# Linear-recurrence stage with its decay exponents as TensorE products and its heads interleaved

## What is computed

```python
def hgrn2_mixer(hq, hf, hi, hg, lb, out_gain):
    log_f = logaddexp(log(lb), log1p(-lb) + log_sigmoid(hf))
    k = -expm1(log_f)
    q = silu(hq)
    o = hgrn2_chunk_scan(q, k, hi, log_f)      # per head
    return rmsnorm(o, out_gain) * silu(hg)

# S_t = diag(f_t) S_{t-1} + k_t v_t^T,  o_t = S_t^T q_t, in chunks:
def step(S, (qi, ki, vi, gi)):
    b = cumsum(gi)
    o_inter = einsum('tk,kv->tv', qi * exp(b), S)
    att = einsum('tk,tsk,sk->ts', qi, exp(b_t - b_s where s <= t), ki)
    o_intra = att @ vi
    S_new = exp(b_last) * S + (ki * exp(b_last - b))^T @ vi
```

## Time and profile before

| | |
|---|---|
| three timed runs, median (lowest to highest) | 2146.06 us (2145.73 to 2147.39) |
| the profiled execution's own time | 2147.82 us |
| its span, first to last instruction | 2146.0 us |
| TensorE, VectorE, ScalarE, POOL busy | 1964.3, 1076.2, 739.0, 98.7 us |
| mean granted clock of TensorE | 0.955 |
| recurrence and first `wout` tile | 252.97 to 409.06 us |

### The profile page before, as it was taken

The page is one execution under the profiler, slowest core; times in us unless marked ns, Lnnn a source line. Parts: engine busy times, 40 slices in busy tenths (PEclk is TensorE's granted clock), DMA queues, the critical chain, the costliest instruction groups (busy, mean ns, idle before and its releaser), DMA issues.

```text
span 2146.0 us, 28165 instructions
## 1 busy us (share of the span) xinstructions
PE 1964.3 (92%) x11116; PEld 1695.4 (79%) x11116; DVE 1076.2 (50%) x1469; ACT 739.0 (34%) x1185; POOL 98.7 (5%) x106
## 2 busy tenths in 40 slices
PE   7999765799999998799999999999787989999996
PEld 7878665799999998688888877777587758888884
DVE  4643477444443446854444557676525253323334
ACT  4352333133323233342232334534435242212221
POOL 0100144100000000000000000000000020000000
PEclk9999878899999999999999999999979989999998
DMA  4211000133232322323323322222001313223221
GB/s 171 69 50 49 30 1 0 49 88 90 89 90 81 97 89 66 101 89 98 97 89 98 93 84 89 69 69 79 30 1 44 104 49 98 90 90 104 90 94 44
DMA packets 45475, 161.28 MB, mean 75 GB/s; under 512 B 4848, under 2 KB 5104, under 8 KB 45232
## 3 DMA queue, kind: packets, MB, share of 16 engines
q1 hardware_dynamic: 45216, 158.60, 23.4%
q10 hardware_dynamic: 144, 1.05, 0.1%
HBM read 155.43 MB, written 4.19 MB: 74 GB/s over the span
## 4 chain that ended last, share of the span: by engine, by line
PE 85%; DVE 7%; ACT 4%; issue 2%; DVEq 1%; DMA 0%; ACTq 0%; SPq 0%; POOL 0%; POOLq 0%
PE ps L466 72%; PE ps L836 2%; PE ps L588 2%; DVEq L1946 1%; PE ps L756 1%; PE ps L856 1%; PE ps L729 1%; DVE XE L1942 1%; DVE wlo L1778 1%; DVE W L2088 1%; PE ps L727 1%; DVE GT L2394 1%; PE ps L999 0%; DMA raw<-W 0%; ACT RR L1675 0%
## 5 line engine op out<-in xcount | busy, mean ns | idle before, releaser
L466 PE MATMUL ps<-UH,whi 128*128 128x264 f32 (+1 forms) x1888 | 653.2, 346 | 32.2 <-issue 15.4
L466 PE MATMUL ps<-UL,whi 128*128 128x264 f32 (+1 forms) x1888 | 644.1, 341 | 0.1
L466 PE MATMUL ps<-UH,wlo 128*128 128x264 f32 (+2 forms) x1600 | 527.8, 330 | 0.0
L1178 ACT ACTIVATE whi<-raw 128x1024 fp32r<-128x1024 f32 x284 | 297.4, 1053 | 469.5 <-PE ps L466 449.6
L466 PEld LDWEIGHTS ps<-UH,whi 128*128 128x128 f32 x1888 | 361.4, 191 | 83.4 <-issue 18.0
L466 PEld LDWEIGHTS ps<-UL,whi 128*128 128x128 f32 x1888 | 361.2, 191 | 41.0 <-issue 2.3
L1778 DVE TENSOR_TENSOR wlo<-raw,whi 128x1024 fp32r<-128x1024 f32 x248 | 302.1, 1221 | 52.0 <-ACT whi L1178 51.9
L466 PEld LDWEIGHTS ps<-UH,wlo 128*128 128x128 f32 (+1 forms) x1600 | 305.7, 191 | 27.0 <-issue 0.2
L466 PE MATMUL ps<-HH,whi 128*128 128x264 f32 (+1 forms) x768 | 246.4, 321 | 0.0
L466 PE MATMUL ps<-HL,whi 128*128 128x264 f32 (+1 forms) x768 | 246.3, 321 | 0.0
L466 PE MATMUL ps<-HH,wlo 128*128 128x264 f32 (+1 forms) x768 | 245.7, 320 | 0.0
(11 more groups left out here) (359 smaller groups left out, 2422.1 us busy)
## 6 DMA issues: line engine op xcount, KB each, us to landing
raw<-W SPq DMA_DIRECT2D x284, 512.0 KB, 3.5
H<-xT SPq DMA_DIRECT2D x4, 528.0 KB, 6.7
spill<-H SPq DMA_DIRECT2D x1, 2048.0 KB, 7.1
H<-spill SPq DMA_DIRECT2D x1, 2048.0 KB, 8.7
out<-H SPq DMA_DIRECT2D x8, 256.0 KB, 2.0
MEM<-memT ACTq DMA_DIRECT2D x1, 1024.0 KB, 4.9
masks<-masks SPq DMA_DIRECT2D x1, 768.0 KB, 9.1
TAB<-rope SPq DMA_DIRECT2D x1, 264.0 KB, 12.8
```

The lines of the kernel that those rows point to most:

```text
L466: mm = pe.matmul(dst, a, b, start=start and n == 0, stop=stop_ and n == 2)
L1178: act.activation(whi[s % NB][:, :, :], raw[s % NB][:, :, :], ACT.Copy).then_inc(w_hi, 1)
```

## The change

The meta tokens of all four heads become one compact part of 64 columns (`MT`), and the frames four chunks of 128, 512 columns a head. The exponents no longer come from POOL: ScalarE copies the turned logs out of PSUM rounded (`LTH`), VectorE makes the rest (`LTL`), and TensorE multiplies both by a table of ones (`MF`, ten 128 x 128 masks from the constants, loaded late over ScalarE's queue), which gives four levels' exponents in one go of 512 columns a chunk (`hgrn_decays`), and the running sums by a product of 128 columns (`hgrn_sums`). ScalarE's exponentials read them from PSUM. Keys and queries are multiplied by their decays on VectorE, as the norm is by the gate. POOL has no part in it. `hgrn_log` and `hgrn_key` stand inside the attention, on ScalarE and VectorE. The hardware loops are written out, and the end of head h (outputs, norm, gate) stands between the levels of head h + 1. The `wout` tiles take the attention's blocks first and wait head by head.

```diff
-NCH = LP // CH
+NCH = 5
...
+MT = 4 * META
...
-            def hgrn(h, more):
-
-                def w(name, per, c, h=h):
-                    pool.wait_ge(X[name], count(X, name, h * per + c))
-
-                def diff(l):
-
-                    m = CH >> l
-                    left, right = halves(bb, m)
-                    ref = left[:, :, m - 1:m].to_broadcast([P, LP // (2 * m), m])
-                    dl, dr = halves(XD[l % 2], m)
-                    if l >= 3:
-                        w("E", LEVELS, l - 2)
-                    pool.tensor_tensor(dl, ref, left, ALU.subtract)
-                    pool.tensor_tensor(dr, right, ref, ALU.subtract).then_inc(X["D"], 1)
...
-                w("k", 1, 1)
-                w("b", 1, 1)
-                for l in range(1, LEVELS + 1):
-                    diff(l)
-                    if l == 4:
-                        pool.drain()
-                        w("eb", 1, 1)
-                        pool.tensor_tensor(qb[:, P:LP], qp[:, P:LP], TB[:, 0:4 * P], ALU.mult).then_inc(X["qb"], 1)
-                    if l == 5:
-                        w("ek", 1, 1)
-                        pool.tensor_tensor(kd[:, 0:4 * P], kp[:, 0:4 * P], kd[:, 0:4 * P], ALU.mult
-                                           ).then_inc(X["kd"], 1)
-                if more:
-                    w("vtc", 1, 1)
...
+            def hgrn_decays(h, half):
+                pe.wait_ge(X["ltl"], h + 1)
+                if half:
+                    pe.wait_ge(X["E"], LEVELS * h + 4)
+                elif h:
+                    pe.wait_ge(X["E"], LEVELS * h)
+                    pe.wait_ge(X["dk"], h)
+                for c in range(4):
+                    pe.matmul(ps[:, c, :], LTH[h % 2][:, c, :], MF[:, 4 * half:4 * half + 4, :], start=True, stop=False)
+                    mm = pe.matmul(ps[:, c, :], LTL[h % 2][:, c, :], MF[:, 4 * half:4 * half + 4, :], start=False, stop=True)
+                mm.then_inc(X["D"], 1)
...
+            def hgrn_sums(h):
+                pe.wait_ge(X["vtc"], h + 1)
+                for c in range(4):
+                    pe.matmul(ps[:, 6, c * P:(c + 1) * P], LTH[h % 2][:, c, :], MF[:, 8, :], start=True, stop=False)
+                    mm = pe.matmul(ps[:, 6, c * P:(c + 1) * P], LTL[h % 2][:, c, :], MF[:, 8, :], start=False, stop=True)
+                mm.then_inc(X["D"], 1)
...
+            def hgrn_scores(h, l):
+                if l == 0:
+                    pe.wait_ge(X["k"], h + 1)
+                    a, b = ZH[:, 8 + h, META:L], ZH[:, h, META:L]
+                else:
+                    pe.wait_ge(X["EQ"], LEVELS * h + l)
+                    a = b = XE[l % 4]
+                if 8 * h + l >= 2:
+                    pe.wait_ge(X["am"], 8 * h + l - 1)
+                for c in range(4):
+                    mm = pe.matmul(ps[:, 4 + l % 2, c * P:(c + 1) * P], columns(a, c), columns(b, c), start=True, stop=True)
                 mm.then_inc(X["A"], 1)
...
+            def hgrn():
+                hgrn_logs_turned(0)
+                meta_logs_turned()
+                hgrn_decays(0, 0)
+                meta_decays()
+                for h in range(HEADS):
+                    hgrn_scores(h, 0)
+                    hgrn_decays(h, 1)
+                    if h == 1:
...
+                    hgrn_scores(h, 5)
+                    if h == 0:
+                        hgrn_sums(0)
+                    else:
+                        hgrn_keys_turned(h)
+                    hgrn_scores(h, 6)
+                    if h == 0:
+                        hgrn_keys_turned(0)
+                    else:
+                        hgrn_states(h)
+                    if h + 1 < HEADS:
+                        hgrn_decays(h + 1, 0)
+                    if h == 0:
...
+                    hgrn_scores(h, 7)
+                    if h == 0:
+                        hgrn_states(0)
+                hgrn_outputs(HEADS - 1)
+                hgrn_norm(HEADS - 1)
...
-            with pe.Fori(0, HEADS) as h:
-                hgrn(h)
...
+            def mixed(e):
+                def hook(k):
+                    if e == 0 and k == 0:
+                        pe.wait_ge(M["end"], HEADS)
+                    if e == 0 and k == HEADS:
+                        pe.wait_ge(MX["dve"], 6)
+                    if e == 0 and k >= HEADS:
+                        pe.wait_ge(X["end"], k - HEADS + 1)
+                return hook
...
+                tile(KT, L, lambda k: u((k + HEADS) % KT), lambda k: ul((k + HEADS) % KT), before=mixed(e))
...
+            def hgrn_log(h):
+                f = ZH[:, 8 + h, :]
+                if h:
+                    act.wait_ge(X["d"], h)
+                act.wait_ge(*evacuated(FT["z%d" % (8 + h)]))
+                act.activation(T1[:, :], f, ACT.Abs)
+                act.drain()
+                act.activation(T1[:, :], T1[:, :], ACT.Exp, scale=-1.0)
+                act.drain()
...
+                    act.activation(ZH[:, 4:8, :], ZH[:, 4:8, :], ACT.Copy, scale=vecs[:, g:g + 1]).then_inc(X["silu"], 1)
...
+                if x in (6, 8, 10, 12):
+                    hgrn_log(x // 2 - 3)
+                if x in (9, 11, 13, 15):
+                    hgrn_key(x // 2 - 4)
+                if x == 16:
+                    act.dma_start(MR[:, :, :], masks_d[:, LEVELS + 5:LEVELS + 15, :]).then_inc(x_in[2], 16)
+                if x == 18:
+                    act.wait_ge(x_in[2], 32)
+                    act.activation(MF[:, :, :], MR[:, :, :], ACT.Copy)
...
+            def hgrn_exp(h, l):
+                act.wait_ge(X["D"], 3 * h + (1 if l <= 4 else 2))
+                if LEVELS * h + l > 4:
+                    act.wait_ge(X["A"], 8 * h + l - 3 if l > 4 else 8 * (h - 1) + (5 if l == 4 else 6 + (l - 1)))
+                i = (l - 1) % 4
+                act.activation(XE[l % 4][:, :].rearrange("p (c t) -> p c t", c=4), ps[:, 0:4, i * P:(i + 1) * P], ACT.Exp
+                               ).then_inc(X["E"], 1)
...
+                if x in (7, 9, 11, 13):
+                    hgrn_log(x // 2 - 3)
...
+            def hgrn_weigh(h, l):
+                m = CH >> l
+                dve.wait_ge(X["E"], LEVELS * h + l)
+                left, right = halves(XE[l % 4], m)
+                dve.tensor_tensor(left, left, halves(ZH[:, 8 + h, META:L], m)[0], ALU.mult)
+                dve.tensor_tensor(right, right, halves(ZH[:, h, META:L], m)[1], ALU.mult).then_inc(X["EQ"], 1)
...
+            def hgrn_keep(h, l):
+                dve.drain()
+                dve.wait_ge(X["A"], 8 * h + l + 1)
+                dve.sem_inc(passed, 1)
+                msk = level[:, l - 1, :].rearrange("p (a t) -> p a t", a=1).to_broadcast([P, 4, P]).bitcast(U32)
+                dve.copy_predicated(by_chunk4(AM[h % 2][:, :]), msk, by_chunk4(ps[:, 4 + l % 2, :])).then_inc(X["am"], 1)
...
+            def hgrn_key_decay(h):
+                dve.wait_ge(X["dk"], h + 1)
+                dve.tensor_tensor(ED[:, 0:3 * P], ED[:, 0:3 * P], ZH[:, 8 + h, META:META + 3 * P], ALU.mult
+                                  ).then_inc(X["kd"], 1)
+            def hgrn_query_decay(h):
+                dve.wait_ge(X["eb"], h + 1)
+                dve.tensor_tensor(QB[h % 2][:, :], QB[h % 2][:, :], ZH[:, h, META:L], ALU.mult).then_inc(X["qb"], 1)
...
-            def hgrn_decays(h):
...
-                for c in range(NCH):
-                    last = dve.tensor_tensor_scan(bb[:, c * P:(c + 1) * P], ones, lf[:, c * P:(c + 1) * P], 0.0,
-                                                  ALU.mult, ALU.add)
...
+                hgrn_keep(h, 2)
+                hgrn_key_decay(h)
+                hgrn_weigh(h, 4)
+                hgrn_keep(h, 3)
+                if h:
+                    hgrn_gated(h - 1)
+                else:
+                    mla_lo(2)
...
+            hgrn_gated(HEADS - 1)
+            hgrn_lo(HEADS - 1)
...
+    for l in range(1, LEVELS + 1):
+        m = CH >> l
+        block, right = s // m == t // m, t % (2 * m) >= m
+        masks.append(block & np.where(right, s <= t, s > t))
+    masks += [s > t, s <= t, (s // META == t // META) & (s > t)]
```

548 lines of the change are left out of this document (338 added, 210 removed).

## The result

The changed kernel takes 2078.2 us (median of 4 runs, 2075.2 to 2081.1), the kernel before 2146.7 in the same session: a ratio of 0.968, with an interval of 0.966 to 0.970. That is 68 us less; the forecast was 52 less, 2095 us, with a range from 2083. The profiled execution took 2075.2 us, and its span is 2073.4 us.

What follows compares the result with a forecast made beforehand. VectorE was taken to bound the changed heads: entry 8, three heads 60.3, last 17.5, meta 2, end 8.6, low clock 6.5, waits 1 make 104 us against 156.1, 52 less. Forecast 2095 us, range 2083 to 2113.

Steps and rivals of the forecast that it cites:

- Weightings and copies: VectorE in each head: 14 weightings at 0.41 us without POOL beside them, seven masked copies at 0.74 us.
- A head of 20.1 us: Recurrence stage: 16.6 us of VectorE work plus 3.5 us of idling ahead of masked copies make one head's period.
- The mechanism of the head: VectorE's work and hand-overs set a head's 20.1 us; TensorE stays under it with 17.8 us at the upper clock.
- Meta tokens: Head 0: 18 small VectorE instructions for the compact part of 64 columns, net +2 us.
- Last head: Last head of the recurrence stage, with no next head's work in it: 17.5 us.
- End: Last outputs, norm and first `wout` tile: 8.6 us, with 42 of the tile's 48 products under TensorE's wait.
- Low clock for half a head, +6.5: Recurrence stage: TensorE at the lower clock for half a head in all, adding 6.5 us.
- unnamed waits, +1: Recurrence stage: 1 us added for waits that the sum doesn't name.
- Attention: Logarithms, key exponentials and scaled copies moved into the attention cost 0 there, with bounds of -0.5 and +4 us.
- The rest of the kernel: Everything outside the recurrence stage: no change in time, so the whole 52 us gain lies in the stage.
- better than the sum: Rival: gaps ahead of masked copies filled, 2 us a head, and no low clock; 2081 us, under 2087, chance 0.12.
- two other rivals: Nothing gained: heads of 33 to 35 us, chance 0.03; slower: heads from about 37 us, 2154 at 39, chance 0.02.

Runs made afterwards that it cites:

- pool_back: Changed kernel with unused POOL subtractions and multiplications put back into the recurrence stage; the stage grew by 19.3 us.
- wout_plain: Changed kernel with the output projection's products in plain order, the first tile behind all heads; stage 5.1 us longer, median time 5.6 us longer.
- after: The changed kernel itself, as profiled: 2078.2 us, median of 4 runs.
- no_interleave: Changed kernel with each head's output part back at the end of its own head instead of inside the next; the stage took 20.3 us more.
- logs_late: Changed kernel with the four heads' logarithms and key exponentials moved behind the attention; attention ended at 250.7 us, the stage took 17 us more.
- before_unrolled: Kernel before the change with TensorE's hardware loop over the four heads written out; ratio 0.9993 to the kernel before, stage 156.1 us.
- before: The kernel before the change: 2146.7 us in the same session as the changed kernel.
- pe_less: Changed kernel without the low part's products for the exponents, so decays are less exact; 2078.8 us, stage 88.3 us.
- pe_less_pad: Same as pe_less, but with a 2-column product in place of each one left out; 2074.0 us, stage 90.9 us.
- early_tile: Changed kernel with 24 products of the first `wout` tile ahead of the last head's outputs and 6 between outputs and norm; stage 2.7 us shorter.
- pe_extra: Changed kernel with the running sums' TensorE products done three times per head; 4.5 us more over three heads, stage 1.9 us longer.
- split_products: Changed kernel with each block of exponent products done in two halves of 256 columns; stage 92.3 us, 3.3 us shorter.

## Why the prediction missed

The forecast was 52 us of gain, all in the stage. Of the 68 measured, 60 lie in the stage and 8 outside. Two steps failed by that much: 7.5 us for the lower clock and unnamed waits in the stage, and nothing for the rest of the kernel. With either one put right, the forecast's range from 2083 us would have begun at about 2075 us.

- *Entry*, 8 us: 8.0, at a granted clock of 0.79.
- *Weightings and copies*: 0.42 for 0.41 us, 0.73 for 0.74; POOL as their brake is shown by `pool_back`.
- *A head of 20.1 us* fails as a size: 18.7 without the meta part. The forecast's 16.6 us of VectorE work are right as a sum of recorded lengths (14 x 0.418 + 7 x 0.734 + 6 x 0.685 + 0.54 + 3 x 0.347 = 16.7), but VectorE was busy for 14.93, since the lengths overlap by 0.08 to 0.10 us at most hand-overs (a weighting that starts at 298.50 us has the next behind it at 298.83, and is recorded with 0.42). I had seen that overlap and then left it in the sum as something to spare instead of taking off its 1.6 us. The Trainium skill's "VectorE: DVE Perf Modes", section "The DRAIN you can't avoid", says that the next operation does not start until the pipeline is empty. The trace does not agree as far as recorded starts and lengths go (298.83 us is 0.09 us before the recorded end), and the 2101 us of that rule were the worse answer.
- *The mechanism of the head* was only half right. I had VectorE's work and hand-overs as the bound and TensorE under it. The 3.8 us of VectorE's idle time matched the 3.5 by chance: 2.8 are left ahead of the copies, 0.7 is a wait for an exponential, which the sum left out (2.5 us a head before), and TensorE's microseconds turned out to be on the chain.
- *Meta tokens*, +2: 1.9 us in each of two heads, 3.8.
- *Last head*, 17.5: 16.7.
- *End*, 8.6: 11.3. The last outputs ran at the lower clock, 3.5 us for the 2.0 of the sum, and the 48 products of 0.12 us don't fit under the wait as I had them: TensorE is busy with them for all 6.4 us, and 1.55 us of that are left behind the last low part instead of 0.7. That the order of the products hides 5 us or more is shown by `wout_plain`.
- *Low clock for half a head, +6.5*, *and unnamed waits, +1*: this is the step that failed by most in the stage. The granted clock was 1.00 in all four heads, in both profiles of after. I had carried over the mean of a stage in which TensorE waits for 10.5 us a head into one in which it doesn't. I had also read these as waits ahead of 14 groups of `L588`; they were four, one of them 6.3 us. In the changed kernel the longest in the heads is 1.2 us. Where the waits come back (2.85 us in `no_interleave`) the clock is down again. With it the stage's 8 us are made up: 7.5 here, 4.2 in three heads and 0.8 in the last, less 1.8 for the meta tokens and 2.7 at the end.
- *Attention*, 0: nothing in `logs_late` or `before_unrolled` speaks against it, within a scatter of several us that goes with the clock.
- *The rest of the kernel*, 0: wrong by 8.1 us in the mean of the runs (2146.9 against 2078.7, less 60.1). It was put at nothing because the change doesn't touch it. Part of it is TensorE's wait at the exit of the first MLP's loop, which went with the hardware loop over heads: behind the first tile TensorE idles 96.3 us before and 90.4 after. That `before_unrolled` lost this wait and gained nothing shows how little of it need reach the time. The remainder is not settled: among kernels whose code behind the stage is the same, that part took 1728.7 to 1734.3 us without the wait, as the granted clock fell at other places, and the attention ended anywhere from 248.1 to 255.0 us.

The rival "better than the sum", 2081 us, was nearest. Of its two reasons the clock held; the gaps ahead of the copies shrank by 0.7 us a head instead of 2. The figures of two other rivals don't agree with each other: one has a head of 34 us as today's time, the other breaks even at about 37 us, since it takes the last head as shorter and the first does not.

Of the signs named in advance, the weightings, the empty POOL, the clock over 0.9 and the place of the tile's first products came. The tile ended at 344.6 us, not near 357, VectorE was busy for 14.9 to 16.7 us of 18.7 to 20.6, and the attention ended 4.3 us early.

## What to carry to other kernels

Add lengths of back-to-back instructions less their overlap, and don't carry a stage's mean clock into one whose waits are gone: ask how long the engine will sit idle at one place, and leave room, for even that doesn't settle it: a wait of about 2.6 us ahead of the last outputs was followed by the lower clock in seven profiles here and by the upper one in three. An engine's busy share doesn't say whether its work is on the chain; adding the same work at two places and on two engines does. And a change that alters the number of instructions can move a wait hundreds of microseconds away, so cut profiles into lengths before a difference in time is explained, and look at the granted clock of each length.

## What the runs showed of the hardware

- TensorE waited 2.4 to 3.9 us at the exit of a hardware loop in two programs (`before` twice, `pe_less`) and not in 14 profiles of others with the same code at that place; `pe_less` and `pe_less_pad` differ only in 2-column products ahead of it.
- POOL holds up a VectorE multiplication whose two operands lie in the same memory as its own (0.42 us to 1.01 in the mean, 1.49 at most), and not a masked copy that reads one operand from `ps` (0.734 and 0.737).
- A product of 256 columns follows the one before after 0.12 us, one of 512 after 0.23, one of 128 after 0.11, and one of 2 adds 0.11: below 256 columns width costs next to nothing here.
- Waits of 2.9 us (`early_tile`) and of 2.6 us ahead of the last outputs (`after` and six others) were followed by the lower clock. The same wait, 2.5 to 2.6 us, was not in `pe_extra`, `pe_less_pad` and `split_products`, nor were waits of up to 1.2 us inside the heads of `after`. What tips it is not shown.
